# Five feed-forward norms take their mean on all partitions and their root at full width

## The reference

```python
def rmsnorm(x, g):
    xf = x.astype(jnp.float32)
    y = xf * lax.rsqrt(jnp.mean(xf * xf, axis=-1, keepdims=True) + EPS)
    return (y * g.astype(jnp.float32)).astype(x.dtype)

def conv_glu_ffn(h, w_up, conv_w, conv_b, w_down):
    u = causal_dwconv(jnp.einsum('btd,df->btf', h, w_up), conv_w, conv_b)
    gate, val = jnp.split(u, 2, axis=-1)
    return jnp.einsum('btf,fd->btd', jax.nn.silu(gate) * val, w_down)
...
        h = h + conv_glu_ffn(rmsnorm(h, norm_ffn_g[l]), ...)
...
        x = x + 0.5 * _swiglu_ffn(_rmsnorm(x, ffn1_norm[i]), ffn1_w_gate_up[i], ffn1_w_down[i])
```

## Time and profile before

| | |
|---|---|
| Median of 3 runs | 3874.89 us (3868.4 to 3875.88) |
| Profiled execution | 3872.72 us |
| Its span, first to last instruction | 3870.9 us |
| TensorE busy | 3680.0 us, 95% |
| VectorE, ScalarE, GpSimd busy | 1766.4, 1150.3, 1341.4 us |
| Mean granted TensorE clock | 0.955 of full |

### The profile page before, as it was taken

How to read it: one execution, slowest core, us unless ns; L and a number is a source line. 1 busy time by engine, 2 the same in 40 slices (tenths; PEclk the granted TensorE clock), 3 DMA queues, 4 the chain that set the end, 5 groups by cost and what they waited for, 6 DMA issues and landing times.

```text
span 3870.9 us, 55899 instructions
## 1 busy us (share of the span) xinstructions
PE 3680.0 (95%) x20870; PEld 3142.3 (81%) x20870; DVE 1766.4 (46%) x2440; ACT 1150.3 (30%) x1622; POOL 1341.4 (35%) x530
## 2 busy tenths in 40 slices
PE   7999999999999999999998878999999989899999
PEld 7994999989958999978876656888788868777887
DVE  4343552552434525552458774424542453634242
ACT  4333332324333323321222243212222223532121
POOL 3210343433102343344433301444344434334443
PEclk9996999999978999999999878999999999999999
DMA  3210232322101333223322201333233323222332
GB/s 109 61 45 0 71 93 87 93 70 81 38 14 50 89 90 90 84 87 93 97 82 65 65 1 44 92 94 98 85 94 93 101 82 92 71 76 87 98 92 92
DMA packets 570031, 294.79 MB, mean 76 GB/s; under 512 B 10663, under 2 KB 568230, under 8 KB 569782
## 3 DMA queue, kind: packets, MB, share of 16 engines
q1 hardware_dynamic: 568724, 291.39, 25.8%
q0 software_dynamic: 768, 1.11, 0.1%
q10 hardware_dynamic: 418, 0.62, 0.0%
HBM read 291.00 MB, written 2.10 MB: 76 GB/s over the span
## 4 chain that ended last, share of the span: by engine, by line
issue 49%; PE 39%; POOL 10%; DVE 1%; ACT 0%; POOLq 0%; DMA 0%; SPq 0%; ACTq 0%; DVEq 0%
PE big L1717 34%; POOL wlow L634 10%; PE big L1758 1%; PE misc L1906 1%; PE misc L1889 1%; POOLq L176 0%; DVE fresh L1233 0%; DMA load_xin<-in_x 0%; PE misc L1822 0%; DVE acc L1152 0%; PE misc L1782 0%; DVE mix_lev L1401 0%; PE misc L1899 0%; PE misc L1936 0%; PE misc L1771 0%
## 5 line engine op out<-in xcount | busy, mean ns | idle before, releaser
L634 POOL TENSOR_TENSOR wlow<-raw,whigh 128x1024 fp32r<-128x1024 f32 (+1 forms) x508 | 1331.1, 2621 | 2497.7 <-ACT whigh L648 2497.7
L648 ACT CAST whigh<-raw 128x1024 fp32r<-128x1024 f32 (+1 forms) x508 | 564.0, 1110 | 2158.7 <-PE big L1717 2044.1
L1717 PE MATMUL big<-xhigh,whigh 128*128 128x512 f32 (+1 forms) x2160 | 680.3, 351 | 0.6 <-POOL wlow L634 0.3
L1717 PE MATMUL big<-xlow,whigh 128*128 128x512 f32 (+1 forms) x2160 | 673.0, 348 | 0.0
L1717 PE MATMUL big<-xhigh,wlow 128*128 128x512 f32 (+1 forms) x2160 | 670.4, 347 | 0.0
L1717 PE MATMUL big<-ffn_x2l,whigh 128*128 128x264 f32 (+1 forms) x2016 | 540.1, 322 | 0.0
L1717 PE MATMUL big<-ffn_x2h,whigh 128*128 128x264 f32 (+1 forms) x2016 | 537.5, 321 | 2.1 <-DVE ffn_zg L1309 2.1
L1717 PE MATMUL big<-ffn_x2h,wlow 128*128 128x264 f32 (+1 forms) x2016 | 538.2, 321 | 0.0
L1717 PEld LDWEIGHTS big<-xhigh,whigh 128*128 128x128 f32 x2160 | 378.2, 190 | 62.2 <-issue 7.4
L1717 PEld LDWEIGHTS big<-xlow,whigh 128*128 128x128 f32 x2160 | 376.5, 189 | 57.3 <-issue 5.6
L1717 PE MATMUL big<-ffn_hidl,whigh 128*128 128x264 f32 (+1 forms) x1408 | 421.4, 340 | 0.0
(11 more groups left out here) (335 smaller groups left out, 3753.5 us busy)
## 6 DMA issues: line engine op xcount, KB each, us to landing
raw<-in_ffn_w_gate_up SPq DMA_DIRECT2D x176, 512.0 KB, 3.8
raw<-in_ffn_w_down SPq DMA_DIRECT2D x96, 704.0 KB, 4.7
raw<-in_ffn_w_up SPq DMA_DIRECT2D x88, 512.0 KB, 3.8
raw<-in_w_in SPq DMA_DIRECT2D x52, 512.0 KB, 3.8
raw<-in_gmlp_w_in SPq DMA_DIRECT2D x32, 512.0 KB, 4.1
raw<-in_attn_w_in SPq DMA_DIRECT2D x24, 512.0 KB, 3.8
raw<-in_w_out SPq DMA_DIRECT2D x16, 512.0 KB, 4.0
raw<-in_gmlp_w_out SPq DMA_DIRECT2D x16, 512.0 KB, 3.9
```

Of the source, the lines that this page charges most:

```text
L634: eng.tensor_tensor(wlow[:, at0:at0 + n], raw[:, at0:at0 + n], whigh[:, at0:at0 + n].bitcast(F32), ALU.subtract).then_inc(slab_split, 1)
L648: eng.copy(whigh[:, at0:at0 + w], raw[:, at0:at0 + w]).then_inc(high_rounded, 1)
L1717: mm = eng.matmul(wide(big, slot, T)[:, c:c + n], w[:, (s * KC + k) * P:(s * KC + k + 1) * P], x[:, (x0 + k) * width + c:(x0 + k) * width ...
```

## The change

For the five feed-forward norms that do not follow the final norm, TensorE multiplies a full 128 by 128 matrix of 1/1024 with `acc` (`spread`, L1808): this sums over the partitions and leaves the mean of every token on all 128 partitions at once. VectorE takes the root of that at full width, 528 or 512 columns, straight into `rstd`, with `acc` as scratch; steps one, three and seven read the means from PSUM, the other six read SBUF alone. The spread at step 8 and the copy are gone for these five. The final norm keeps the old way, and so do the norms ahead of the mixers, attention and gMLP. Counters replace the norm's index where the semaphores of spread and width are waited for.

```diff
+            def norm_wide(j, T):
+
+                eng.wait_ge(ms_done, j + 1)
+                root(rstd[:, 0:T], wide(misc, 0, T), EPS, rstd_wide)
+                eng.wait_ge(rstd_wide, widths[0] + 1)
+                widths[0] += 1
...
                 if ph[0] in ("cffn", "ffn"):
                     if plan[n - 1][0] != "final":
-                        norm_root(norm_of[n], norm_T[norm_of[n]])
+                        norm_wide(norm_of[n], norm_T[norm_of[n]])
...
-                    if n is not None and step == SPREAD_AT:
+                    if n is not None and step == SPREAD_AT and plan[n - 1][0] == "final":
                         norm_spread(n)
...
+            def spread(dst, mat, src, T):
+                for c, n in parts(T):
+                    mm = eng.matmul(dst[:, c:c + n], mat, src[:, c:c + n], start=True, stop=True)
+                return mm
...
-                mm = column_means(misc, 0, "mean1024", acc, T)
                 if plan[n - 1][0] == "final":
+                    column_means(misc, 0, "mean1024", acc, T)
                     eng.wait_ge(summed2, 9)
                     mm = column_means(misc, 4, "mean1024", acc2, T)
+                elif n in x_of:
+                    mm = spread(wide(misc, 0, T), square("mean1024"), acc, T)
+                else:
+                    mm = column_means(misc, 0, "mean1024", acc, T)
                 mm.then_inc(ms_done, 1)
```

More of the change, by code:

```diff
@@ L1152, in add_squares @@
                 eng.tensor_tensor(acc[:, 0:T], acc[:, 0:T], c1(sqr, s, T), ALU.add).then_inc(summed, 1)
-            roots = [0]
+            roots, spreads, widths = [0], [0], [0]
             def root(dst, src, eps, done, tmp=acc, ahead=None):
@@ L1193, in norm_root @@
                 root(rcol[:, 0:len(blocks(T))], misc[:, 0:len(blocks(T))], EPS, rstd_ready, rcol2)
-                eng.wait_ge(rstd_spread, j + 1)
+                eng.wait_ge(rstd_spread, spreads[0] + 1)
                 eng.tensor_copy(rstd[:, 0:T], by_block(misc, 0, T)).then_inc(rstd_wide, 1)
-                eng.wait_ge(rstd_wide, j + 1)
+                spreads[0] += 1
+                eng.wait_ge(rstd_wide, widths[0] + 1)
[3 more added lines that the diff above has]
+                root(rstd[:, 0:T], wide(misc, 0, T), EPS, rstd_wide)
+                eng.wait_ge(rstd_wide, widths[0] + 1)
+                widths[0] += 1
             def low_of(n, k, T):
@@ L1785, in row_spread @@
                 return mm
+            def spread(dst, mat, src, T):
+                for c, n in parts(T):
+                    mm = eng.matmul(dst[:, c:c + n], mat, src[:, c:c + n], start=True, stop=True)
+                return mm
+            spreads = []
             def norm_means(n):
@@ L1799, in norm_spread @@
                 T = norm_T[j]
-                eng.wait_ge(rstd_ready, j + 1)
+                spreads.append(n)
+                eng.wait_ge(rstd_ready, len(spreads))
                 mm = row_spread(misc, 0, 0, T)
@@ L1804, in norm_spread @@
                 mm.then_inc(rstd_spread, 1)
[L1806 to L1809, removed]
             eng.wait_ge(squares_in, 16)
```

## The result

| | before | after |
|---|---|---|
| Median | 3874.89 us (5 runs, 3868.40 to 3876.04) | 3895.78 us (5 runs, 3893.97 to 3901.26) |
| Profiled execution, span | 3872.72, 3870.9 us | 3901.26, 3899.5 us |
| Mean granted clock | 0.955 | 0.949 |

The ratio is 1.0065, 95% interval 1.0054 to 1.0076: 25 us slower by the ratio, while the two medians lie 20.9 us apart. 3900 was predicted, in a range of 3884 to 3909. The profiled execution is the slowest of the five.

The account below looks back on a forecast made before the run. TensorE was taken as the bound, without idle time in the last feed-forward stage. Later second pairs (15.8 us) and clock falls (5 x 2.3 = 11.5) add 27.3 to 3872.7: 3900 us, range 3884 to 3909.

Parts of the forecast that it names:

- The product: Full-matrix product on TensorE in five norms: 0.86 us at 512 columns, 0.89 at 528, replacing 1.79 and 2.22.
- The length of the root and the hold: VectorE's nine wide steps take 6.24 us; the sixth, held by GpSimd's subtraction, ends 0.55 us after it.
- rival B: Sixth root step starts before GpSimd's subtraction, eighth is held instead: 3886 to 3893 us, chance 0.13.
- The delay of the second pair: TensorE starts the second pair of tiles later: +2.88 us at 512 tokens, +3.59 at 528, in five stages.
- the sum: Five changed places: 15.8 us of later second pairs plus 11.5 for the clock, together +27.3 us, 0.7%.
- The clock: TensorE's clock falls behind each of the five stalls, costing 2.3 us each, 11.5 us together.
- rival C: The clock stays up behind the stalls, so only 15.8 us are added: 3889 us, chance 0.10.
- Rival D: No stall: the root stays under the first pair of tiles and 5.5 us are saved: 3867 us, chance 0.06.

Follow-up runs that it names:

- the run with the means at step 3: The changed kernel with the means' product of the five norms issued at step 3 of the first pair instead of step 6: ratio 0.9989, median 3868.00 us.
- the early small root: The kernel before, with the five norms' means at step 3 and spread at step 5 instead of 6 and 8: ratio 1.0005.
- the second's: The changed kernel as it is, measured once more for a second profile, against the kernel before: ratio 1.0078 [1.0064, 1.0092].
- A delay alone: The kernel before with four idle products behind the first pair of tiles of each of the five stages, TensorE working, no stall added: ratio 1.0037.

## Why the prediction was right

- **The product.** It occupies 0.86 us at 512 columns as worked out (3521.36 to the second product behind it, 3522.45, less 0.23), and the root starts 1.05 us after the product (1.06 taken from attention), 1.08 at 528 columns (1.09).
- **The length of the root and the hold.** Sixth step, in all five places, as forecast; rival B (the step gets in first) did not happen even at a margin of 0.06 to 0.09 us. With one of its two inputs in PSUM instead of SBUF the step took 0.69 us.
- **The delay of the second pair.** +2.88 and +3.59 us, to the hundredth what the sum had. The stalls are 3.64 and 5.99 where 3.81 and 6.15 were worked out: the profile counts idle time from the modelled end of the last product, 0.16 later than its issue interval.
- **The clock.** It fell to 0.50 behind all five stalls, so rival C is out. But no run shows the 2.3 us that the sum has for each: they are the author's estimate, the middle of 1.7 and 3.0, which are halves of the two stretches of the earlier trace rows. What the traces show in its place is 3.4 us at 0.50 behind each stall, 1.7 us. Five times that is 8.5 for 11.5. With 15.8 it makes 24.3; the five stages together grew by 21.5. Most of the difference is a term that the sum did not have: at the beginning of the five stages, behind the stalls that were there already, TensorE worked 18.3 us at the lower level in this profile in place of 23.2, which gives about 2.5 us back.
- **Rival D** needed the root under the first pair. It is true of the run with the means at step 3, which is 0.1% faster than before. The saved work of 5.5 us, which the prediction let stand only under D, is what that run gains over the early small root: 0.0016 or 6 us.

That 3900 lies so near the 3896 measured is in part luck. The sum had 27.3 us in the five places, where the profiles have 21.5 and 21.4; the ratios, 25 and 30 us, hold some 4 to 9 us beside them for which the sum had no term. Against them stand the clock's term, too large by 3, and the 2.5 given back at the beginnings, so the two errors nearly cancel.

What stays open is this rest. The first ratio's interval (21 to 29 us) still holds 21.5, the second's (25 to 36) does not, so over many executions a part of the rest may belong to the change; one profile cannot tell, as the unchanged stages vary by as much without it. A delay alone (1.0037 for 1.0040 expected) did not bring such a cost.

## What to carry to other kernels

Moving a small computation to full width trades work on the busy engine for length on the chain: before doing it, lay the chain's steps end to end against the work that covers them, and if they stick out, start the chain earlier; here three steps earlier turned +0.65% into -0.1%. A stall cost its length here (3.64 us at the last stage) and, where the clock fell to 0.50 behind it, about 1.7 us more, and the two can be priced apart by filling the stall with idle work (8.1 us less over the five). Lay the chain beside GpSimd's instructions as well: here a step that reads SBUF alone and came just behind one of them waited for nearly all of it (the sixth step, 2.86 us for 0.69).

## What the runs showed of the hardware

**Steps of VectorE beside GpSimd's subtraction.** In the changed kernel a step with both inputs in SBUF that started 0.06 to 0.09 us behind the subtraction lasted 2.85 to 2.90 us and ended 0.55 to 0.57 us after it; with its scratch in PSUM the same step, with one input there, started 0.09 behind and took 0.69. The kernel before shows the other order too: in attention the eighth step of a root starts at 2046.41, 0.03 us ahead of a subtraction, and keeps its 0.69, while the subtraction takes 2.92 us instead of 2.40. A small step was held as well: one of 128x4, 0.16 us alone, lasted 2.19 when it started 0.18 behind a subtraction (1646.19, before the final norm's spread). So was one with a single input, in SBUF: the second step takes 0.43 alone and lasted 2.28 at 2040.47, 0.41 behind a subtraction.

**The clock behind a stall.** In front of the second pair of the changed stages stalls of 1.49 to 1.50 us (three, in one run) were followed by a clock of 1.00, and those of 3.63 to 6.00, in all runs that have them, by 0.50. No length between was seen there. The clock's record and the pace of the products can disagree: at the beginning of the kernel before, behind a stall of 4.43 us that ends at 31.95, it reads 1.00 until 60, yet the ten products of the column means take 2.29 us there, as much as at 836.12, where it reads 0.50, and not the 1.17 of 447.51. Pairs of issues of 264 columns start 0.44 us apart there (43.34 and 43.78), 0.24 from 48.72 on.
